# Gate and up loops of 512 tokens: two weight sums move to PSUM, the gating's accumulators share a bank, and the first tile is issued in another order

## The reference

```python
def swiglu(x, w_in, w_out):
    gu = x @ w_in
    return (jax.nn.silu(gu[..., :D_FF]) * gu[..., D_FF:]) @ w_out          # D_FF = 2816

h = h + 0.5 * rmsnorm(swiglu(rmsnorm(h, gn[0]), ffn_w_in[i, 0], ffn_w_out[i, 0]), gn[1])   # 528 tokens
...                                                                        # mLSTM mixer
h = h + 0.5 * rmsnorm(swiglu(rmsnorm(h, gn[4]), ffn_w_in[i, 1], ffn_w_out[i, 1]), gn[5])   # 512 tokens
...
h = h + 0.5 * swiglu_2(rms_norm(h, ffn1_norm[l]), ffn1_w_gate[l], ffn1_w_up[l], ffn1_w_down[l])
...                                                                        # attention and retention
h = h + 0.5 * swiglu_2(rms_norm(h, ffn2_norm[l]), ffn2_w_gate[l], ffn2_w_up[l], ffn2_w_down[l])
```

## Time and profile before

| | |
|---|---|
| median of 3 runs | 1971.41 us (1967.55 to 1973.95) |
| profiled execution, its own time | 1965.56 us |
| its span, first to last instruction | 1963.8 us |
| PE busy | 1914.4 us (97%) |
| DVE busy | 1448.7 us (74%) |
| ACT busy | 1024.6 us (52%) |
| POOL busy | 889.5 us (45%) |
| mean granted TensorE clock | 0.995 of full |

### The profile page before, as it was taken

How to read it: one execution, slowest core, us unless ns; L and a number is a source line. 1 busy time by engine, 2 the same in 40 slices (tenths; PEclk the granted TensorE clock), 3 DMA queues, 4 the chain that set the end, 5 groups by cost and what they waited for, 6 DMA issues and landing times. The chain is left out here.

```text
span 1963.8 us, 38283 instructions
## 1 busy us (share of the span) xinstructions
PE 1914.4 (97%) x13945; PEld 1758.1 (90%) x13945; DVE 1448.7 (74%) x1936; ACT 1024.6 (52%) x1695; POOL 889.5 (45%) x525
## 2 busy tenths in 40 slices
PE   8999999999999999999999999999999999999998
PEld 8999999997779899989989998897775678999898
DVE  5976787785456987777788778777666548877876
ACT  5566654525224566664546666445245445666543
POOL 3454453634335455553635556244441044555533
PEclk9999999999999999999999999999999999999999
DMA  6233324322312233333323333343211022333332
GB/s 177 65 107 103 93 85 117 88 58 75 108 55 64 82 112 107 99 94 102 104 75 108 106 106 110 86 114 106 72 53 43 1 86 75 108 107 103 101 87 86
DMA packets 344605, 178.05 MB, mean 91 GB/s; under 512 B 18715, under 2 KB 340118, under 8 KB 344494
## 3 DMA queue, kind: packets, MB, share of 16 engines
q1 hardware_dynamic: 342640, 175.46, 31.3%
q10 hardware_dynamic: 1854, 1.07, 0.2%
HBM read 174.42 MB, written 2.10 MB: 90 GB/s over the span
## 5 line engine op out<-in xcount | busy, mean ns | idle before, releaser
L3402 PE MATMUL ps<-xop,whi 128*128 128x256 f32 (+1 forms) x4032 | 724.6, 282 | 14.2 <-ACT wa L848 7.8
L3402 PEld LDWEIGHTS ps<-xop,whi 128*128 128x128 f32 x4032 | 622.1, 189 | 16.9 <-POOL wlo L595 8.5
L3402 PE MATMUL ps<-xop,wlo 128*128 128x256 f32 (+1 forms) x2016 | 568.7, 282 | 0.0
L536 POOL TENSOR_TENSOR wlo<-raw,whi 128x1024 fp32r<-128x1024 f32 x94 | 234.2, 2500 | 378.7 <-ACT whi L700 373.6
L595 POOL TENSOR_TENSOR wlo<-raw,whi 128x512 fp32r<-128x512 f32 x212 | 292.4, 1383 | 219.9 <-ACT whi L830 219.8
L3402 PEld LDWEIGHTS ps<-xop,wlo 128*128 128x128 f32 x2016 | 380.4, 189 | 0.0
L830 ACT ACTIVATE whi<-stage 128x512 fp32r<-128x512 f32 x216 | 136.6, 632 | 207.9 <-DVE stage L1936 131.1
L3340 PE MATMUL ps<-xop,whi 128*128 128x256 f32 (+1 forms) x896 | 215.4, 284 | 6.6 <-DVE hT L2126 1.8
L3079 PE MATMUL ps<-xhi,whi 128*128 128x512 f32 (+2 forms) x624 | 210.9, 367 | 1.4 <-DVE xlo L1832 1.2
L3079 PE MATMUL ps<-xlo,whi 128*128 128x512 f32 (+2 forms) x624 | 204.6, 357 | 0.0
L3079 PE MATMUL ps<-xhi,wlo 128*128 128x512 f32 (+2 forms) x624 | 204.2, 356 | 0.0
(11 more groups left out here) (463 smaller groups left out, 3995.9 us busy)
## 6 DMA issues: line engine op xcount, KB each, us to landing
raw<-in_ffn_w_in SPq DMA_DIRECT2D x88, 512.0 KB, 3.7
raw<-in_ffn_w_gate SPq DMA_DIRECT2D x44, 512.0 KB, 3.6
raw<-in_ffn_w_up SPq DMA_DIRECT2D x44, 512.0 KB, 3.7
raw<-in_ffn_w_out SPq DMA_DIRECT2D x32, 512.0 KB, 4.1
raw<-in_ffn_w_down SPq DMA_DIRECT2D x32, 512.0 KB, 4.4
raw<-in_a_w_in SPq DMA_DIRECT2D x24, 512.0 KB, 3.9
raw<-in_w_in SPq DMA_DIRECT2D x19, 512.0 KB, 3.8
raw<-in_ffn_w_out SPq DMA_DIRECT2D x16, 384.0 KB, 3.5
```

The source lines that it names most:

```text
L536: pool.tensor_tensor(wlo[:, u % SLOTS, :], raw[:, u % SLOTS, :], whi[:, u % SLOTS, :].bitcast(F32), ALU.subtract).then_inc(lo_done, 1)
L3402: ins = pe.matmul(ps[:, bank_, 0:h], w[l][:, k * P:(k + 1) * P], x[r][:, k * h:(k + 1) * h], start=start and k == 0 and q == 0, stop=k == ...
```

## The change

For the three layers of 512 tokens:

- S2 is written to PSUM bank 4 and S4 to bank 1 (`sum_place`), no longer to SBUF. Their high and low parts are made from there.
- To free these banks M2 and M5 (with M3 added) share one bank, in columns 0 to 255 and 256 to 511: bank 5 in even tiles, 2 in odd ones. Only M5, the first to write there, starts the bank; M2 is written without the start flag. PE's wait for the kept M5 moves from M3 to M2, and in the loop ACT keeps M5 ahead of the high part of the next A11.
- S4 waits until ACT has read S2 (its high part), since both read bank 4.
- In tile 0 DVE's order is S2, low of S2, S4, S3, then the activations' low part and the low of S4; the conv tile's last multiply moves behind the next tile's S1. ACT keeps M5 and M6 there ahead of the next A21 and A11.
- In the last tile ACT keeps M5 ahead of the high parts of the hidden tiles.

For the first layer (528 tokens) only one thing moves: in tile 0 ACT keeps M6 ahead of the high part of the next S1. The core of the diff:

```diff
         def body(st):
...
+            a, d = acc_part(c, n, "M1"), acc_part(c, n, "M5")
             hi_sum(st, "S4", "M3")
             if not first:
                 keep(st, "M1", kept(n)[:, 0, :], a, done(i, "gate", before(st)))
             hi_sum(st, "S3", "M7")
             if not last:
-                keep_a21(nxt)
-                hi_a11(nxt)
-            else:
+                if not first or n == TOK:
+                    keep_a21(nxt)
+                if n == TOK:
+                    hi_a11(nxt)
+            elif n == TOK:
                 hid_hi(0, 4)
             keep(st, "M5", m5_of(n), d, None if first else done(i, "c22", before(st)))
+            if n == SEQ:
+                if last:
+                    hid_hi(0, 4)
+                elif not first:
+                    hi_a11(nxt)
+            if first:
+                keep(st, "M6", kept(n)[:, 1, :], a, None)
+                if n == SEQ:
+                    keep_a21(nxt)
+                    hi_a11(nxt)
...
             hi(st, "A22", raw_blocks(i, c)["A22"], "M4")
-            keep(st, "M6", kept(n)[:, 1, :], a, None)
+            if not first:
+                keep(st, "M6", kept(n)[:, 1, :], a, None)
...
+    def acc_part(c, n, product):
+
+        h = half_of(n)
+        if n == SEQ:
+            a, bd = ((3, 5), (0, 2))[c % 2]
+            return dict(M1=ps[:, a, 0:h], M2=ps[:, bd, 0:h], M5=ps[:, bd, h:2 * h])[product]
+        return ps[:, 3 * (c % 2) + dict(M1=0, M2=1, M5=2)[product], 0:h]
...
+    def sum_place(i, name):
+
+        if FFNS[i]["n"] == SEQ and name in ("S2", "S4"):
+            return ps[:, 4 if name == "S2" else 1, :]
+        return ps[:, 7, :] if name == "S1" else operand(stage, i, name)
...
             v.wait_ge(*done(i, "S2", st))
-            v.tensor_tensor(operand(stage, i, "S4"), raw_blocks(i, st[1])["A12"], operand(stage, i, "S2"), ALU.subtract) \
+            if n == SEQ:
+                v.wait_ge(*done(i, "hi_S2", st))
+            v.tensor_tensor(sum_place(i, "S4"), raw_blocks(i, st[1])["A12"], sum_place(i, "S2"), ALU.subtract) \
              .then_inc(s["w_sum"], 1)
...
                 s1(nxt)
+                if first and n == SEQ:
+                    conv_last(3)
                 lo(nxt, "S1")
...
         s2(start)
-        s4(start)
-        lo(start, "S2")
-        x_lo(4, 5)
-        lo(start, "S4")
-        s3(start)
-        conv_up(3)
-        x_lo(5, 6)
+        if n == SEQ:
+            lo(start, "S2")
+            s4(start)
+            s3(start)
+            x_lo(4, 5)
+            lo(start, "S4")
+            conv_product(3)
+            x_lo(5, 6)
...
             pe.wait_ge(*done(i, "lo_A12", st))
-            multiply("A12", b, True).then_inc(s["mult"], 1)
+            if n == SEQ:
+                pe.wait_ge(*done(i, "m5_kept", st))
+            multiply("A12", b, n == TOK).then_inc(s["mult"], 1)
             pe.wait_ge(*done(i, "lo_S4", st))
-            pe.wait_ge(*done(i, "m5_kept", st))
+            if n == TOK:
+                pe.wait_ge(*done(i, "m5_kept", st))
             multiply("S4", d, False).then_inc(s["mult"], 1)
```

More of the change, by code:

```diff
@@ L841, in hi_sum, with keep @@
             act.wait_ge(*done(i, name, st))
-            hi(st, name, ps[:, 7, :] if name == "S1" else operand(stage, i, name), product)
-        def keep(st, product, dst, bank_, free):
+            hi(st, name, sum_place(i, name), product)
+        def keep(st, product, dst, source, free):
             act.wait_ge(*done(i, product, st))
@@ L847, in keep @@
                 act.wait_ge(*free)
-            act.activation(dst, ps[:, bank_, 0:h], ACT.Copy).then_inc(s["kept"], 1)
+            act.activation(dst, source, ACT.Copy).then_inc(s["kept"], 1)
         def hid_hi(first, last):
@@ L906, in act_ffn @@
         hi((None, 0), "A12", raw_blocks(i, 0)["A12"], "M2")
-        keep((None, 0), "M1", kept(n)[:, 0, :], acc_banks(0, n)[0], (c_s["banks_free"], c_at["banks_free"] + NCONV + 1))
+        keep((None, 0), "M1", kept(n)[:, 0, :], acc_part(0, n, "M1"), (c_s["banks_free"], c_at["banks_free"] + NCONV + 1))
         body((None, 0))
@@ L1974, in gate @@
             v.wait_ge(c_s["hid"], count(c_at["hid"] + NCONV, st))
[L1975 removed]
+            v.tensor_tensor(gates_of(n), gate_parts(c, n), kept(n), ALU.add).then_inc(s["gate"], 1)
         def hidden(st):
             r, c = st
[L1980 removed]
+            a = acc_part(c, n, "M1")
             if r is None and c == NFAST - 1:
@@ L2057, in dve_ffn @@
         s2(start)
-        s4(start)
-        lo(start, "S2")
-        x_lo(4, 5)
-        lo(start, "S4")
-        s3(start)
-        conv_up(3)
-        x_lo(5, 6)
+        if n == SEQ:
[6 more added lines that the diff above has]
+            x_lo(5, 6)
+        else:
+            s4(start)
+            lo(start, "S2")
+            x_lo(4, 5)
+            lo(start, "S4")
+            s3(start)
+            conv_up(3)
+            x_lo(5, 6)
         body(start)
@@ L3394, in pe_fast, with multiply @@
         c_s, c_at, h = ffn_s, ffn_at[i], half_of(n)
-        def multiply(name, bank_, start):
+        def multiply(name, to, start):
             w = [operand(buf, i, name) for buf in (whi, wlo)]
@@ L3413, in m4 @@
             pe.wait_ge(*done(i, "c22", st))
-            ins = multiply("A22", acc_banks(c, n)[0], False)
+            ins = multiply("A22", acc_part(c, n, "M1"), False)
             if last:
@@ L3421, in body @@
             r, c = st
-            a, b, d = acc_banks(c, n)
+            a, b, d = [acc_part(c, n, product) for product in ("M1", "M2", "M5")]
             first = r is None and c == 0
```

31 lines of the change are left out of this document (17 added, 14 removed).

## The result

The changed kernel takes 1956.09 us (median of 4 runs, 1954.51 to 1958.62) against 1970.63 us for the kernel before beside it; the ratio is 0.9942, with a 95% interval of 0.9924 to 0.996. The profiled execution took 1955.32 us, its span 1953.5. The forecast was 1965.3 us, from a range of 1959.5 to 1970.5, so the direction was right and the size was not: 6 us were forecast, and a little over 10 came.

A forecast was written before the change was run, and what follows sets the result against it. PE, busy 97% of the span, bounds the kernel; in tile 0 DVE's queue to C22 holds M4. Chains of 5.5 us and clock of 0.6 gave 1971.4 - 6.1 = 1965.3 us, range 1959.5 to 1970.5.

The forecast's parts named there:

- the base: Starting time: the runs' median, 5.85 us above the profiled execution, was kept, so 1971.4 - 6.1 = 1965.3 us.
- the turns with POOL: Tile 0, second layer: DVE's overlaps with POOL's low parts after the change, 0.11, 0.16, 0.76 and 0.73, together 1.76 us.
- the clock: Third layer's lower-clock stretch, 1.25 us lost; shorter stops should make it rarer, so half was counted, 0.6 us.
- the sum: Whole kernel: layers' gains 2.1 + 2.1 + 1.2 + 0.05 = 5.5 us of chains and 0.6 of clock, 6.1 us.
- what is late next: Tile 0: M4 needs C22, last in DVE's queue, so the gain is what DVE's queue gains; 1.85 us in the second layer.
- the rival that all waits go: Tile 0: if C22 did not hold M4, 11.3 us would be gained, 1960.1 us; chance 0.12.
- the small terms: Among them: first layer gains 0.05 us; tile 1's M6, no longer held by S2's low part, gives 0.27 in the second.
- M2's new wait: M2 now waits for the kept M5; costed at nothing. As slower rival: 0.2 us late gives 1975 us, chance 0.10.
- the rule that was weighed there: Skill's 58 fixed cycles from SBUF, 120 from PSUM: 0.26 us a layer, sum 4.8 us; the trace does not show it.
- The margin of 1.6 us for M2: Tile 8: M2 started at about 751.2, the kept M5 ended at 750.14, and the change makes M5 0.5 us earlier.
- M6's share: Tile 1: M6 no longer held by S2's low part, 0.27 us in the second layer, 0.28 in the fourth.
- In tiles 2 to 17 nothing: Second layer's loop: PE busy 158.93 of 159.00 us over 16 tiles, so shorter DVE or POOL instructions there are worth nothing.

The follow-up runs named there:

- M6 sooner: Kernel before with one edit, ACT keeping M6 right behind M5 in tile 0 of all four layers: 1966.94 us, ratio 1.0005.
- either half alone: Changed kernel with S2 and S4 back in SBUF: 1962.8 us, ratio 0.9976; changed kernel with the order of before on DVE and ACT: 1962.65 us, ratio 0.9984.
- the conv multiply back: Changed kernel with the conv tile's last multiply beside its first again: 1961.91 us, ratio 0.9969.
- the two later comparisons: Changed kernel, unchanged, against the kernel before on other chips: 1957.48 us, ratio 0.9941, and 1956.29 us, ratio 0.994.
- one instruction moved: Changed kernel with the third activations' low part behind the next S2 and the gate in 512-token loops: 1953.5 us, ratio to before 0.9927.

## Why the prediction was right in direction and wrong in size

The path was right: what holds M4 next, and that the gain is what DVE's queue gains. The step that failed most is the base, "I keep the difference", worth 4.1 us. With the base right the forecast would have been 1961.2 and still 4 us too high, because its gain was too small: what the turns with POOL give back by 1.1 us, the clock by 1.7, and by 1.4 for the spacing of the matmuls, which the sum put at nothing.

**Right: what is late next.** PE's stops ahead of M3 and M7 went, one of 1.63 us ahead of M4 came (2.0 forecast), put down to C22 at the end of DVE's queue. M6 sooner without a shorter queue gave nothing (ratio 1.0005), so the rival that all waits go is out.

**Right: the small terms.** First layer 0.05 forecast, 0.06 measured (16.01 to 15.95); M6 of tile 1 no longer held by the low part of S2; M2's new wait shows a stop in one of twelve loops in four traces of the changed kernel (0.41 us, in tile 1 of the fourth layer), and none in tiles 2 to 17; the low parts of S2 and S4 last 0.69 us from PSUM, so the extra charge of the rule that was weighed there isn't seen (three times 0.26 off 5.5 is also 4.7, not 4.8). PE stays busy in tiles 2 to 17. The margin of 1.6 us for M2 was read in tile 8, though. In tile 1 M2 starts 16.09 us after the loop's first matmul in the second layer and the kept M5 ends at 15.84, a margin of 0.25; costing it at nothing there was in part luck.

**Mis-sized: the turns with POOL.** The step counted 1.76 us of turns after and 10.6 + 0.97 + 1.76 = 13.3 for the queue. The trace has 0.51 + 0.76 = 1.27 and 12.88: the two of 0.11 and 0.16 cost nothing, though the instructions stand where the step put them (POOL's low part of A12 ends at 665.60 + 1.29 = 666.89, DVE's part starts at 666.77 and still takes 1.22), and the conv multiply's was 0.51 for 0.76. The step counted each overlap in full. But it had itself read that DVE's part ends 1.1 us behind POOL's, and alone it takes 1.21, so the first 0.11 us of an overlap cost nothing. Worked that way its four overlaps give 0, 0.05, 0.65 and 0.62, 1.3 us, and 12.9 for the queue, which is what came; rows of the fourth layer agree (the conv multiply overlaps by 1.27 and is 1.14 longer). With M6's share the second and third loop gained 2.51 us each for 2.12, the fourth 1.55 for 1.2 (15.54 to 13.98 or 14.02). Chains in all: 0.06 + 2.51 + 2.51 + 1.55 = 6.6 us where the sum had 5.5.

**Mis-sized: the clock.** The sum counted half of one stretch, 0.6 us. Three traces before have five of them in twelve loops' starts, which cost 1.24 (18.44 - 17.20), 1.49, 1.63, 1.25 and 1.28 us, 6.9 in all or 2.3 for an execution. Four traces after have none in sixteen. Over the first 20 us of the loops in all the traces here it is 10 in 28 for the kernels whose PE stops for 2.7 us or more in all in tiles 0 and 1 of the second and third layer (before, M6 sooner, either half alone, the conv multiply back) and 0 in 36 for the others. Each of the ten begins 0.2 to 1.5 us behind the end of a stop of 1.75 us or more. In these loops none begins behind a stop of 1.7 us or less, nor behind most of the longer ones. The Trainium skill, "TensorE: Matmul & The Clock Gate", section "What's actually happening", puts the clock down to TensorE's activity, and this agrees in direction. That the shorter stops are what keeps the clock up is the likeliest reading; no run here set the length of a long stop alone, so it isn't shown.

**Missed: the spacing.** "In tiles 2 to 17 nothing" was right for DVE and POOL, but the loop's matmuls come at one of two spacings. Windows of PE in the second layer's loop, from the first trace after and from the second:

```profile
690.00:840.00 150.00, 150.00 (x1276) 1.00 0.35 102
```

```profile
690.00:840.00 150.00, 150.00 (x1268) 1.00 0.35 102
```

With the same instructions and the full clock, 1276 or 1268 matmuls fall in 150 us: 0.1176 and 0.1183 us each by this count, which takes in those cut by the window's ends, and 0.1178 and 0.1185 from start to start. A tile takes 9.893 or 9.956 us, and 17 of them differ by 1.07 us. A loop stays in one or the other to its end. Before, 7 of 9 of the 512-token loops had the slower one, after, 4 of 12; that is 2.33 against 1.0 loops an execution, 1.4 us. Other kernels with long stops had it in 0 of 3 loops twice and in 1 of 3 twice, so this may be chance, and 1.4 us of the gain with it. Its cause stays open.

**Wrong: the base.** The step kept the 5.85 us by which the median of three runs stood above the profiled execution. With more runs the kernel before takes 1966.9 to 1968.1 us, 4 us less than 1971.4. On the usual time, 1967.3, the same sum would have given 1961.2. The profiled execution that the prediction had beside it, 1965.56, lay nearer to the usual time: from it the sum gave 1958.8.

Together: measured about 1957 us, forecast 1965.3. Of the 8.3 us between them 4.1 are the base (1971.4 to 1967.3), 1.1 the turns, 1.7 the clock and 1.4 the spacing. The measured gain, 10.2 and 10.6 us in the medians of the two later comparisons, is met by 6.6 + 2.3 + 1.4 = 10.3. The traces check this sum: from first to last matmul the four loops take 739.8, 742.9 and 740.9 us together before and 729.9, 731.8, 731.8 and 729.4 after, 10.5 us less in the mean. All the rest of the program takes 1225.1 before and 1226.6 after in the mean (1224.6 without the fourth trace, the one with the long stop in the mixer), so no other stage brought anything to speak of. With three and four traces the clock's and the spacing's shares are rough.

## What to carry to other kernels

Before a wait is counted as a gain, follow it to the next thing that is late: a stop of 2 us was removed alone, and the time stayed. Where two engines take turns, don't price a new order by the average turn; write both engines' starts side by side, because moving an instruction of 0.6 us changed the queue by 1.8, count only the part of an overlap that the rows show to cost, and then look for the place at which the turn falls away, which by traces and medians gave another 2.8 us for one instruction moved. Where two such starts fell within 0.04 us the order differed from execution to execution, and 1.1 us with it. When the late thing is sooner, look at the next one again: here it is the kept M5 ahead of M2 in tile 1, with 0.25 us to spare. And take a base from as many runs as can be had: the median of three was off by 4 us, where a gain of 6 was forecast.

## What the runs showed of the hardware

A DVE instruction of 1024 columns with both inputs in SBUF takes 1.22 us alone, and when one of POOL's that reads SBUF is running, it ends 1.1 us behind that one's end, after 2.3 us at the most beside one of 512 columns; beside a fill by POOL, which reads nothing, it keeps 1.22 us. The fill itself takes 0.53 us for 512 columns where the subtraction takes 1.28.

TensorE ran whole loops of 170 us at either of two spacings of its 128x256 matmuls, 0.1178 or 0.1185 us, at full granted clock and without any stop. The same program had either one in the same loop in different executions.

Stretches at TensorE's lower clock came in lengths of 3.41 us or twice that in every trace, but for the last one of the program, and one in tile 0 or 1 of a loop cost 1.2 to 1.6 us.
